# A mixture-of-experts layer: third expert asked for earlier, shared products by features, one recurrent product moved, gate products on four row groups

## What is computed

```python
def reference(x, c, ...):
    mod = (silu(c) @ ada_w + ada_b)
    sh1, sc1, g1, sh2, sc2, g2 = split(mod, 6)
    u = _rmsnorm(x, norm1_g) * (1 + sc1) + sh1
    h = x + g1 * _mixer(u, ...)
    u = _rmsnorm(h, norm2_g) * (1 + sc2) + sh2
    h = h + g2 * _moe(u, ...)
    return _rmsnorm(h, final_g)

def _mixer(u, ...):
    xr = _causal_conv(u @ w_rx, conv_w, conv_b)        # rx, 4 taps
    h_rnn = _rglru(xr, ...)
    y_a = (h_rnn * gelu(u @ w_rg)) @ w_branch_a
    q, k, v = u @ w_q, u @ w_k, u @ w_v
    log_alpha = log_sigmoid((u @ w_lr) @ gla_w_up + gla_b_up) / 16   # w_lr is 1024 x 16
    o = _gla(q, k, v, log_alpha)                       # chunks of 64: state, then o
    y_b = (_rmsnorm(o, gla_norm_g) * silu(u @ w_og)) @ w_branch_b
    return (sigmoid(u @ w_ga) * y_a + sigmoid(u @ w_gb) * y_b) @ w_out

def _moe(u, ...):                                      # 128 experts, 8 for each token
    idx, wts = top_k(sigmoid(u @ router_w) + router_b)
    routed = sum over the 8 experts of wts * _swiglu(u, exp_w_gu[e], exp_w_down[e])
    return routed + _swiglu(u, shared_w_gu, shared_w_down)
```

## Time and profile before

| | us |
|---|---|
| median of 3 runs | 1409.2 (1407.07 to 1409.36) |
| the profiled execution | 1407.99 |
| its span, first to last instruction | 1406.2 |
| TensorE matmul busy | 1351.8 (96% of the span) |
| weight load, DVE, ACT, POOL busy | 995.6, 841.4, 653.9, 192.9 |
| mean granted TensorE clock | 0.976 of full speed |

### The profile page before, as it was taken

One profiled execution on the slowest core, in us unless ns is written; L12 is line 12 of the kernel. 1 busy time (PEld: TensorE's weight loads), 2 busy tenths in 40 slices (PEclk: granted clock), 3 DMA queues, 4 the chain that ended last, 5 costly groups with the idle time before them and its releaser, 6 DMA issues.

```text
span 1406.2 us, 26548 instructions
## 1 busy us (share of the span) xinstructions
PE 1351.8 (96%) x5930; PEld 995.6 (71%) x5931; DVE 841.4 (60%) x1369; ACT 653.9 (46%) x826; POOL 192.9 (14%) x322
## 2 busy tenths in 40 slices
PE   5999999999999999889999999999999999999984
PEld 5678877878888788466777767677676777777631
DVE  4432555955636877766764767766676655464418
ACT  5581236364222313346654656655665545454202
POOL 1000000000000000312222222222222222222200
PEclk9899999999999999999999999999999999999987
DMA  9432111233726752668886869978897685667185
GB/s 341 127 105 60 61 60 60 73 124 103 255 76 237 259 168 93 237 228 295 303 299 221 313 238 349 351 264 307 313 358 261 217 285 203 238 235 239 63 350 196
DMA packets 104618, 301.23 MB, mean 214 GB/s; under 512 B 20490, under 2 KB 23794, under 8 KB 95619
## 3 DMA queue, kind: packets, MB, share of 16 engines
q1 hardware_dynamic: 78706, 258.09, 52.3%
q0 software_dynamic: 20800, 33.61, 7.0%
q10 hardware_dynamic: 5072, 9.02, 1.8%
HBM read 319.51 MB, written 40.90 MB: 256 GB/s over the span
## 4 chain that ended last, share of the span: by engine, by line
PE 87%; DVE 5%; DMA 3%; ACT 2%; issue 2%; SPq 1%; ACTq 0%; DVEq 0%
PE psum L1546 29%; PE psum L1758 25%; PE psum L1799 16%; PE psum L1748 4%; DMA gu_raw<-in_exp_w_gu 3%; PE psum L1519 2%; PE psum L1790 2%; PE psum L1646 1%; PE psum L1687 1%; PE psum L1818 1%; PE psum L1579 1%; DMA ring<-in_ada_w 1%; PE psum L1637 1%; PE psum L1608 1%; DVE gu_lo L1408 1%
## 5 line engine op out<-in xcount | busy, mean ns | idle before, releaser
L1408 DVE TENSOR_TENSOR gu_lo<-gu_raw,gu_hi 128x1024 f32 x204 | 241.3, 1221 | 98.2 <-ACT gu_hi L940 81.8
L940 ACT ACTIVATE gu_hi<-gu_raw 128x1024 f32 x204 | 212.0, 1057 | 117.4 <-DMA gu_raw<-in_exp_w_gu 59.7
L1799 PE MATMUL psum<-w_dn,mask 128*128 x560 | 251.6, 592 | 0.0
L1758 PE MATMUL psum<-gu_hi,xT_hi 128*128 (+1 forms) x568 | 229.7, 404 | 2.6 <-DVE gu_lo L1408 2.3
L1758 PE MATMUL psum<-gu_hi,xT_lo 128*128 (+1 forms) x568 | 223.1, 393 | 0.0
L1758 PE MATMUL psum<-gu_lo,xT_hi 128*128 (+1 forms) x568 | 222.0, 391 | 0.0
L1799 PEld LDWEIGHTS psum<-w_dn,mask 128*128 128x128 f32 x560 | 105.9, 189 | 106.1 <-issue 100.6
L447 DVE TENSOR_TENSOR w_lo<-ring,w_hi 128x1024 fp32r<-128x1024 f32 x80 | 94.6, 1221 | 83.9 <-ACT w_hi L440 82.3
L440 ACT ACTIVATE w_hi<-ring 128x1024 fp32r<-128x1024 f32 x80 | 82.7, 1057 | 125.9 <-PE psum L1546 66.3
L1546 PE MATMUL psum<-uT_hi,w_hi 128*128 128x512 f32 x352 | 139.7, 397 | 1.1 <-DVE w_lo L447 1.1
L1546 PE MATMUL psum<-uT_hi,w_lo 128*128 128x512 f32 x352 | 137.5, 391 | 0.0
(11 more groups left out here) (302 smaller groups left out, 2016.2 us busy)
## 6 DMA issues: line engine op xcount, KB each, us to landing
gu_raw<-in_exp_w_gu SPq DMA_DIRECT2D x208, 512.0 KB, 6.7
w_dn<-in_exp_w_down SPq DMA_DIRECT2D x70, 1024.0 KB
ring<-in_w_in SPq DMA_DIRECT2D x56, 512.0 KB, 5.3
ring<-in_ada_w SPq DMA_DIRECT2D x32, 512.0 KB, 4.8
ring<-expert_rows SPq DMA_DIRECT2D x8, 1024.0 KB, 8.1
ring<-in_ada_w SPq DMA_DIRECT2D x4, 1024.0 KB, 13.4
scale_w<-in_ada_w SPq DMA_DIRECT2D x4, 1024.0 KB, 14.7
ring<-in_w_branch_b SPq DMA_DIRECT2D x8, 512.0 KB, 6.1
```

Of the source, the lines that this page charges most:

```text
L940: act.activation(gu_of(gu_hi, order, p), gu_raw[:, PK * p:PK * p + PK], ACT.Copy).then_inc(gu_hi_ready, 1)
L1408: tt(gu_of(gu_lo, order, p), gu_raw[:, PK * p:PK * p + PK], gu_of(gu_hi, order, p).bitcast(F32), ALU.subtract).then_inc(gu_split, 1)
L1758: mm = pe.matmul(moe_bank(GU), rows[:, s % 2, k], w[:, bass.ds(order % 2, 1), k].rearrange("p o n -> p (o n)"), start=(k == 0 and m == 0), ...
L1799: mm = pe.matmul(moe_bank(Y0 + g), hT[:, j], w_dn[:, bass.ds(order % 3, 1), j, g * NC:(g + 1) * NC].rearrange("p o n -> p (o n)"), start=( ...
```

## The change

1. **Start.** The upper half of the rows of scale half 1 is summed by PE with the weights stationary, and no longer by DVE. ACT makes `full_of(k)` for four k, no longer six, DVE for four. The `w_lr` columns are written four times, 32 columns apart (zeros between), into places of `w_hi` and `w_lo`, so that the job `lr` gives the 16 rows of `lrT` at partitions 0, 32, 64 and 96; `wup` is loaded four times. ACT adds the row of ones as a bias. Gate job t reads partitions 32t to 32t + 16.
2. **Gates.** ACT's Abs, Exp and Ln are done for all four tiles one function after the other.
3. **rx.** Job `rx` 0 goes ahead of the last two `o` jobs; its convolution waits for `o` 7.
4. **Experts.** `load_gu(2)` stands ahead of SP's wait for the last `sgu` job; the loop asks for `load_gu(b + 3)` and `load_down(b + 2)`. `load_down` compares the count of live blocks instead of reading a flag.
5. **Shared expert.** `sgu` job m is 128 features by all 512 tokens (gate, up, gate, up); ACT empties the even ones into `sgate`, DVE the odd ones into `shT`. The transposes, the copy and two waits at the tail go. The shared down products of tiles 2 and 3 stand behind the sums of tiles 0 and 1.

```diff
+        if pair == TT:
+            jobs += [(("rx", 0), "dve")]
...
-        jobs += [(("rx", j), "dve") for j in range(4 * n, 4 * n + 4)]
+        jobs += [(("rx", j), "dve") for j in range(4 * n, 4 * n + 4) if j]
...
-    jobs += [(("sgu", t), "dve") for t in range(TT)]
+    jobs += [(("sgu", m), ("act", "dve")[m % 2]) for m in range(4)]
...
-        wlr_hi = sb("wlr_hi", [P, KT, RANK], F32R, mix)
-        wlr_lo = sb("wlr_lo", [P, KT, RANK], F32R, mix)
-        lrT = oT[0:32, 1, :]
-        wup = oT[0:32, 2, :]
+        wlr_hi = w_lo[:, SPLITS - 1].rearrange("p a (k g r) -> p (a k) g r", g=TT, r=32)
+        wlr_lo = w_hi[:, SPLITS - 1].rearrange("p a (k g r) -> p (a k) g r", g=TT, r=32)
+        wlr_four = wlr[:].unsqueeze(2).broadcast_to([P, KT, TT, RANK])
+        lrT = oT[:, 1, :]
+        wup = oT[:, 2, :]
...
-        sgate = square[:, D - DE:D]
+        sgate = sdown_w[:, 1].rearrange("p (j n) -> p j n", j=2)
...
-        ACT_FULL = (0, 1, 2, 3, 4, 5)
+        ACT_FULL = (0, 1, 3, 5)
...
-            sp.dma_start(wup[0:RANK, :], gla_w_up[0]).then_inc(small_in, 16)
-            sp.dma_start(wup[RANK:RANK + 1, :], gla_b_up).then_inc(small_in, 16)
+            for t in range(TT):
+                sp.dma_start(wup[32 * t:32 * t + RANK, :], gla_w_up[0]).then_inc(small_in, 16)
+                sp.dma_start(wup[32 * t + RANK:32 * t + RANK + 1, :], gla_b_up).then_inc(small_in, 16)
...
-                live = sp.value_load(live_of[0:1, bass.ds(b, 1)], min_val=0, max_val=1)
-                with sp.If(live > 0):
+                with sp.If(live_n > b):
...
+            live_n = sp.value_load(live_count[0:1, 0:1], min_val=1, max_val=MOE_BLOCKS)
+            load_gu(2)
...
             load_down(1, 1)
             for i, s, b in live_blocks(sp, ask=False):
-                load_gu(b + 2)
+                load_gu(b + 3)
                 load_down(b + 2, (s + 2) % UNROLL)
...
+            pool.wait_ge(row_sum, 3)
+            pool.memset(wlr_lo.bitcast(F32), 0.0).then_inc(lr_zero, 1)
...
-            act.activation(lrT[0:RANK, :], bank("lr")[0:RANK, :], ACT.Copy).then_inc(act_emptied, 1)
+            act.activation(lrT, bank("lr"), ACT.Identity, bias=one_row[:]).then_inc(act_emptied, 1)
...
-            def shared_gate(t):
-
-                wait_job(act, ("sgu", t))
-                if t:
-                    wait_emptied(act, ("sgu", t - 1))
-                act.activation(sgate, bank(("sgu", t))[:, 0:DE], ACT.Silu).then_inc(sgate_ready, 1)
+            def shared_gate(j):
+
+                wait_job(act, ("sgu", 2 * j))
...
-            first_hi(range(2))
+            first_hi(range(PIECES))
+            rows_hi(0, 0)
             shared_gate(1)
-            first_hi(range(2, PIECES))
-            rows_hi(0, 0)
-            shared_gate(2)
             act.wait_ge(tables_ready, 1)
             second_hi()
             rows_hi(1, 1)
-            shared_gate(3)
...
-            sum_rows(scale_w[:, 1], scale_in[1], tmpT[:, 1], range(4, KT))
+
+            def full(k):
+                wait_emptied(dve, ("xT", k))
+                own(ts(full_of(k), xnT[:, k], mod_cols[:, KT + k:KT + k + 1], mod_cols[:, k:k + 1], ALU.mult, ALU.add))
+                own.settle()
+
+            full(2)
             for k in range(4):
                 u_lo(k)
+            scale_cols(1)
+            for k in (4, 6, 7):
+                full(k)
             dve.wait_ge(lr_split, 1)
-            tt(wlr_lo[:], wlr[:], wlr_hi[:].bitcast(F32), ALU.subtract).then_inc(lr_split, 1)
-            scale_cols(1)
-            for k in (6, 7):
-                wait_emptied(dve, ("xT", k))
-                own(ts(full_of(k), xnT[:, k], mod_cols[:, KT + k:KT + k + 1], mod_cols[:, k:k + 1], ALU.mult, ALU.add))
-            own.settle()
+            dve.wait_ge(lr_zero, 1)
+            tt(wlr_lo[:, :, :, 0:RANK], wlr_four, wlr_hi[:, :, :, 0:RANK].bitcast(F32), ALU.subtract).then_inc(lr_split, 1)
             for k in range(4, KT):
...
+                if j == 0:
+
+                    wait_job(dve, ("o", NCHUNK - 1))
...
-            def shared_up(t):
-
-                wait_job(dve, ("sgu", t))
-                dve.wait_ge(sgate_ready, t + 1)
-                tt(sh_tok[:, t], sgate, bank(("sgu", t))[:, DE:2 * DE], ALU.mult).then_inc(dve_emptied, 1)
+            def shared_up(j):
+
+                wait_job(dve, ("sgu", 2 * j + 1))
+                wait_emptied(dve, ("sgu", 2 * j))
...
-            columns(("scale", 1), 3, tmpT[:, 1])
+            start_job(("scale", 1))
+            pe.matmul(bank(("scale", 1))[:, 0:4], ident[:], zeros[:, 0:4], start=True, stop=False)
+            pe.wait_ge(scale_in[1][1], 16)
+            for k in range(4, KT):
+                for j in range(4):
+                    pe.matmul(bank(("scale", 1))[:, j:j + 1], scale_w[:, 1, k, j * P:(j + 1) * P], c_col[:, k:k + 1], start=False, stop=False)
+            pe.wait_ge(row_sum, 3)
+            for j in range(4):
+                mm = pe.matmul(bank(("scale", 1))[:, j:j + 1], tmpT[:, 1, j * P:(j + 1) * P], ones[:, 0:1], start=False, stop=(j == 3))
+            end_job(mm)
             pe.wait_ge(lr_split, 2)
...
-                    mm = pe.matmul(bank("lr")[0:RANK, :], w[:, k], acts[:, k], start=(k == 0 and n == 0), stop=(k == KT - 1 and n == 2))
+                    mm = pe.matmul(bank("lr"), w[:, k].rearrange("p g r -> p (g r)"), acts[:, k], start=(k == 0 and n == 0), stop=(k == KT - 1 and n == 2))
...
-                product(("gate", t), lambda k: lrT[0:RANK + 1, t * P:(t + 1) * P], lambda k: wup[0:RANK + 1, :], tiles=1)
+                product(("gate", t), lambda k: lrT[32 * t:32 * t + RANK + 1, t * P:(t + 1) * P], lambda k: wup[32 * t:32 * t + RANK + 1, :], tiles=1)
...
+                else:
+                    split_jobs(("rx", 0), [("rx", 0)], uT_hi, uT_lo, False)
...
-                feature_major(("rx", n))
+                if n == 0:
+                    split_jobs(("rx", 0), [("rx", j) for j in range(1, 4)], uT_hi, uT_lo, False, 1)
+                else:
+                    feature_major(("rx", n))
...
+                at = (t // 2 + 2 * (t % 2)) * P
...
-                    mm = pe.matmul(bank(("sgu", t)), u2T[:, k, t * P:(t + 1) * P], sgu_w[:, k], start=(k == 0), stop=(k == KT - 1))
+                    mm = pe.matmul(bank(("sgu", t)), sgu_w[:, k, at:at + P], u2T[:, k], start=(k == 0), stop=(k == KT - 1))
...
+            wait_emptied(pe, ("sgu", 1))
...
-            for j in range(2):
-                for t in range(TT):
-                    mm = pe.transpose(psum[:, BANKS - 2 + j, t * P:(t + 1) * P], sh_tok[:, t, j * P:(j + 1) * P], ident[:])
-            mm.then_inc(sh_psum, 1)
-            pe.wait_ge(sh_turned, 1)
             pe.wait_ge(shared_in[1], 16)
-            for t in range(TT):
+
+            def shared_down(t):
                 for n in range(2):
                     for j in range(2):
                         pe.matmul(psum[:, 2 * t + n, :], shT[:, j, t * P:(t + 1) * P], sdown_w[:, j, n * NC:(n + 1) * NC], start=(j == 0), stop=False)
+
+            shared_down(0)
+            shared_down(1)
             for t in range(TT):
                 rows = slots_of(t)
                 for r in range(TOP_K // 2):
...
+                if t < TT - 2:
+                    shared_down(t + 2)
```

More of the change, by code:

```diff
@@ L288, in layer_program @@
         lr_split = sem("lr_split")
+        lr_zero = sem("lr_zero")
         o_raw, o_hi_ready, o_split = sem("o_raw"), sem("o_hi_ready"), sem("o_split")
@@ L467, in layer_program @@
         x_rows = x[0].rearrange("(t p) d -> p t d", p=P)
-        SMALL = 3
+        SMALL = 1 + 2 * TT
         VECS = 9
@@ L601, in _ @@
             own(pool.memset(eps[:], EPS))
-            own(pool.memset(lrT, 1.0))
+            own(pool.memset(one_row[:], 0.0))
+            for t in range(TT):
+                own(pool.affine_select(one_row[:], one_row[:], [[0, 1]], ALU.not_equal, 1.0, base=-(32 * t + RANK), channel_multiplier=1))
+            own(pool.memset(wlr_hi.bitcast(F32), 0.0))
             own(pool.affine_select(ident[:], ident[:], [[-1, P]], ALU.not_equal, 1.0, base=0, channel_multiplier=1))
@@ L706, in _ @@
             act.wait_ge(small_in, 16 * SMALL)
-            act.activation(wlr_hi[:], wlr[:], ACT.Copy).then_inc(lr_split, 1)
+            act.activation(wlr_hi[:, :, :, 0:RANK], wlr_four, ACT.Copy).then_inc(lr_split, 1)
             act.wait_ge(cols_ready, 2)
@@ L900, in _ @@
             act.dma_start(row_a[:], final_g.rearrange("(o d) -> o d", o=1).broadcast_to([P, D])).then_inc(fg_in, 16)
-            def shared_gate(t):
-                wait_job(act, ("sgu", t))
-                if t:
-                    wait_emptied(act, ("sgu", t - 1))
-                act.activation(sgate, bank(("sgu", t))[:, 0:DE], ACT.Silu).then_inc(sgate_ready, 1)
+            def shared_gate(j):
+                wait_job(act, ("sgu", 2 * j))
+                act.activation(sgate[:, j], bank(("sgu", 2 * j)), ACT.Silu).then_inc(act_emptied, 1)
             shared_gate(0)
```

(18 more changed lines are left out.)

13 lines of the change are left out of this document (3 added, 10 removed).

## The result

The changed kernel took 1392.8 us (median of 4 runs, 1391.5 to 1394.2), the kernel before beside it 1409.3: a ratio of 0.9887 with a 95% interval of 0.9861 to 0.9914. Forecast were 1390 and 1384 to 1399. The profiled execution took 1393.1 us, its span is 1391.3. Measured again later, beside the kernel before, it gave 1392.4 and 0.9892 (0.9873 to 0.9911).

What follows compares the result with a forecast made beforehand. TensorE (PE), busy in 96% of the span, was taken as the bound. Terms +4.4 - 2.7 - 2.2 - 6.4 - 6.0 - 6.1 = -19.0 us took 1407.99 to 1389.0, stated as 1390 for the median; range 1384 to 1399.

Steps and rivals of the forecast that it cites:

- Start: Before `lr`: PE's new thin products run slow and DVE has more behind them, so `lr` starts at 44.6, 4.4 us lost.
- Gates: Four gate products between the `v` jobs: partial overlap takes 2.1 us instead of 4.82, 2.7 gained; ends 0 and 3.7.
- rx: Job `rx` 0 fills PE's wait for the state before the last `o` jobs, keeping the clock up: 6.4 us gained.
- The bound of 5.5: Upper bound of the loss at the start, if the first weights were late as well: perhaps 5.5 us.
- The 2.2 of slow clock: `v` 1 took 24.01 us against 21.78 for `v` 0; with half the thin work ahead, 2.2 us gained.
- Third expert: Before `gate_up` of block 2: pieces requested 3 to 9 us sooner, 6.0 us gained; ends 3 and 7.1.
- Shared products: Shared expert's `sgu` products: same 32 matmuls, half the evictions at twice the width, where PE has work; nothing gained.
- Tail: After the loop: fewer down products ahead of the first sums, no transposes or copy; 6.1 us gained.
- Late down weights: Rival, in the loop: down loads queue behind `load_gu(b + 3)`, 0.5 us late in each of 51 blocks, 1415; 6%.
- The loads of the fresh run: Rival: loads bind, so PE's lead of block 2 is given back in the next ten blocks, 6 less, 1396; 12%.
- The clock falls: Rival: gates don't overlap and the clock falls behind them, or `o` runs slow: 4.9 or 4.7 less gain, 1394-1395; 20%.
- The cheap start: Rival, at the start: the clock stays up in the new products, 2.6 us more gained, 1387; 12%.

## Why the prediction was right, and where it was not

The forecast of 1390 was 2.8 us below the median, inside the range. For the profiled execution it gave 1389.0, and that took 1393.1. That the sum came so near is in part luck: in the profiled executions the start, the shared weights and the loop were 7.0 us dearer than forecast, and the gates, `rx`, the third expert and the tail 3.0 better.

**Start: sized too low.** The mechanism (PE's thin products at the slow rate on the path to half 1, then DVE's 2.4) is as forecast. The step that failed is "PE is free for them at 36.65 - 4.06 = 32.59", taken from the execution of before. It holds when the clock falls where it fell there: with the same code, other executions had `lr` at 45.2 to 45.4, 0.6 to 0.8 above the forecast of 44.6, with a wait of 0.4 to 0.8 for the weights ahead of the new products in each. In the profiled one the transposes took 0.8 longer and the clock fell earlier, over the products before, and `lr` started at 47.72. The bound of 5.5 was passed in six of nine executions. One of POOL's two new clears does not lie ahead of PE's first product, as the prediction had it, but runs at 33.04, behind DVE's sums; no wait came of it.

**Gates: 2.1 us long failed.** They took 1.07, which is the end of 3.7 gained that the prediction named. The step that failed is "five steps of 0.43": it let neighbouring gates overlap by one record each, as PE issues in order, but the eight records ran in two sets of four, and on two groups in 1.92. The Trainium skill (TensorE: Matmul & The Clock Gate, Part 3) gives 3.07 times for four row groups; the trace agrees, with 3.43 / 1.07 = 3.2 (17 rows here). The 2.2 of slow clock was rightly taken as gained (2.0).

**rx: right**, 6.5 against 6.4, shown by taking the part back.

**Third expert: the gain right, one reason of two wrong.** It was 7.0, near the upper end of 7.1; the lead wasn't given back to the ten fresh blocks, so the discount to 6.0 had no ground. That the last piece hangs on DVE's split was right. That the request moved ahead of the wait for the shared products is what the change says, but a request behind that wait gives the same; the down load and the loop's head ahead of it were the delay.

**Shared products: "nothing" failed**, by 2.7 in the profiled executions. The load's wait wasn't weighed at all: PE waited 1.07 for it in the kernel before, under the cover of DVE's tables. Of the ten executions with the load undivided, nine had it land 12.0 us or more after its request. Why it lands later than the 10.8 before isn't known. The only trace of a reason is that the changed kernels with DVE's sums at the start were as quick as that (10.7, and 9.6 for the second half against 11.0).

**Tail: 6.1 forecast, 6.7 in the mean of twelve executions** (5.8 to 7.4 against 66.0), split 3.0 and 3.7 between the missing steps and the order.

**The rivals.** Late down weights didn't come: no wait for `w_dn` at a down product. The loads of the fresh run didn't bind more than before: from block 2 to the end of the loop the executions took 705.2 to 709.9 us, and that of the kernel before 705.75. The clock falls neither behind the gates nor at `rx`. The cheap start came in no execution.

## What to carry to other kernels

Before moving a request ahead of a wait, read what else stands between the two in that queue: here a load and the loop's head cost 7 us and the wait itself nothing. An engine's short wait can be free while another engine's chain bounds the stage, and still cost through a fall of the clock behind it; price both. Where a stretch of thin products decides the clock, profile more than one execution before a term is sized from it.

## What the runs showed of the hardware

The fall of TensorE's clock is not tied to a place in the program. In one and the same kernel it came before 30 us in one execution and behind 31 in another, and with transposes of 6.05 and 5.33 us ahead of it this moved `v` 0 by 3.6 us. The `tot` job and the two products behind it came in three lengths 1.6 us apart. At the shared weights the clock fell behind a wait of 2.25 us and not behind waits of 2.27 and 2.51. The Trainium skill (TensorE: Matmul & The Clock Gate, Part 1) says that the same kernel measures different numbers of slow matmuls from run to run; the traces agree, with the same 32 transposes at 6.05 and 5.33 us. The granted clock of a row does not show each slow stretch: it reads 1.00 in 24 to 26 for the 11 records of the one execution and for the 19 of the kernel before. The falls at the start and at the gates on one row group began while PE was busy in the whole stretch (2.00 of 2.00) with products of one moving column and of 17 rows, not after a wait.
